# Two fused blocks on one core: one root for two norms, weights split ahead, and the residual's norm moved into the output projection

## The reference, cut to what matters

```python
# end of first_block
x = x + hier_moe(rmsnorm(x, g_ffn), ...)     # 1024 tokens, 1024 features
x = rmsnorm(x, g_final)                      # the "middle" norm
# start of second_block, layer 0
h = rmsnorm_2(x, norm_g[0]) * (1.0 + scale) + shift
proj = h @ w_in[0]                           # many column groups
...                                          # four branches -> y
x = x + gate * (y @ w_out[0])                # needs the normed x of above
```

## Time and profile before

| | before |
|---|---|
| median of 3 runs | 3914.94 us (3911.86 to 3916.8) |
| the profiled execution: time / span | 3911.92 us / 3910.1 us |
| PE busy with matmuls | 3686.8 us, 94% of the span |
| DVE / ACT / POOL busy | 1949.0 / 1546.8 / 69.2 us |
| mean granted TensorE clock | 0.967 of full |
| moved by DMA | 473.83 MB, 121 GB/s over the span |

### The profile page before, as it was taken

One profiled execution on the slowest core, in us unless ns is written; L12 is line 12 of the kernel. 1 busy time (PEld: TensorE's weight loads), 2 busy tenths in 40 slices (PEclk: granted clock), 3 DMA queues, 4 the chain that ended last, 5 costly groups with the idle time before them and its releaser, 6 DMA issues.

```text
span 3910.1 us, 45141 instructions
## 1 busy us (share of the span) xinstructions
PE 3686.8 (94%) x18674; PEld 2905.4 (74%) x18674; DVE 1949.0 (50%) x2538; ACT 1546.8 (40%) x1798; POOL 69.2 (2%) x54
## 2 busy tenths in 40 slices
PE   7999999989999986999999999999999998999998
PEld 5876767766666653777888888787777887788777
DVE  4454544355555534564556653434564456653334
ACT  4331112345555534432455632433433455533333
POOL 0000000000000001000000000000000000000000
PEclk9999999989999997999999999999999999999999
DMA  5101543389999964011101111432010101011232
GB/s 188 44 25 49 174 141 124 111 301 369 373 370 370 367 238 151 29 37 36 54 31 49 35 58 38 151 135 92 33 44 33 55 23 49 33 55 44 104 139 97
DMA packets 92019, 473.83 MB, mean 121 GB/s; under 512 B 10128, under 2 KB 10768, under 8 KB 53920
## 3 DMA queue, kind: packets, MB, share of 16 engines
q1 hardware_dynamic: 77072, 416.32, 29.0%
q0 software_dynamic: 8976, 33.56, 2.2%
q10 hardware_dynamic: 5760, 20.97, 1.3%
HBM read 414.19 MB, written 56.62 MB: 120 GB/s over the span
## 4 chain that ended last, share of the span: by engine, by line
PE 51%; DVE 5%; ACT 4%; issue 2%; ACTq 0%; DVEq 0%
PE ps L136 13%; PE ps L138 13%; PE ps L137 13%; PE ps L1654 3%; PE ps L315 1%; PE ps L1499 1%; PE ps L1479 1%; PE ps L1473 1%; PE ps L1442 1%; PE ps L1899 1%; PE ps L1638 1%; DVE WA L3452 1%; PE ps L3348 0%; PE ps L3381 0%; PE ps L3369 0%
## 5 line engine op out<-in xcount | busy, mean ns | idle before, releaser
L136 PE MATMUL ps<-HH,WS 128*128 128x512 f32 (+1 forms) x2608 | 1055.9, 405 | 25.6 <-DVE HL L3728 17.0
L138 PE MATMUL ps<-HH,WS 128*128 128x512 f32 (+1 forms) x2608 | 1026.6, 394 | 0.0
L137 PE MATMUL ps<-HL,WS 128*128 128x512 f32 (+1 forms) x1968 | 776.5, 395 | 0.0
L136 PEld LDWEIGHTS ps<-HH,WS 128*128 128x128 f32 (+1 forms) x2608 | 496.4, 190 | 156.1 <-issue 33.3
L138 PEld LDWEIGHTS ps<-HH,WS 128*128 128x128 f32 (+1 forms) x2608 | 494.4, 190 | 108.5
L1319 ACT ACTIVATE WA<-ps 128x512 f32<-128x512 f32 x240 | 143.1, 597 | 904.2 <-PE ps L138 794.6
L137 PEld LDWEIGHTS ps<-HL,WS 128*128 128x128 f32 (+1 forms) x1968 | 376.4, 191 | 79.4 <-issue 5.1
L1260 DVE TENSOR_TENSOR WS<-RAW,WS 128x1024 fp32r<-128x1024 f32 (+1 forms) x153 | 200.5, 1311 | 172.4 <-ACT WS L1255 172.3
L136 PE MATMUL ps<-WS,HH 128*128 128x256 f32 x896 | 263.3, 294 | 12.2 <-DVE HL L2131 12.2
L137 PE MATMUL ps<-WS,HH 128*128 128x256 f32 x896 | 256.0, 286 | 0.0
L138 PE MATMUL ps<-WS,HL 128*128 128x256 f32 x896 | 256.0, 286 | 0.0
(11 more groups left out here) (379 smaller groups left out, 5331.2 us busy)
## 6 DMA issues: line engine op xcount, KB each, us to landing
WR<-in_weu SPq DMA_DIRECT2D x37, 1024.0 KB
WR<-in_weg SPq DMA_DIRECT2D x35, 1024.0 KB
WR<-in_wed SPq DMA_DIRECT2D x34, 1024.0 KB
RAW<-in_wo SPq DMA_DIRECT2D x32, 1024.0 KB, 4.9
H<-in_wed SPq DMA_DIRECT2D x26, 1024.0 KB, 8.4
WA<-in_wada SPq DMA_DIRECT2D x48, 512.0 KB
H<-in_weg SPq DMA_DIRECT2D x23, 1024.0 KB, 7.8
H<-in_weu SPq DMA_DIRECT2D x21, 1024.0 KB, 6.4
```

What stands on the lines that cost most here:

```text
L136: t.matmul(o, l[0], r[0], start=st, stop=False)
L137: t.matmul(o, l[0], r[1], start=False, stop=False)
L138: return t.matmul(o, l[1], r[0], start=False, stop=sp)
```

## The change

It has these parts, in order of the program.

1. Routing: the sums of squares of `ffn` are issued one place earlier in PE's list (the sixth ahead of the last product, the seventh ahead of `tensor_row(t, 0)`); `hot` and `places` of k = 1 get the tiles of `PL` and `wrt`. DVE gets 4 instructions for the gains (`vector_gains`) and the bounds in three steps: at the end of the gates, ahead of the wait for the second half of the table, and after expert 0's splits. ACT's bounds stand ahead of expert 0's `start`.
2. The layer's first weights: the rooms `RAW` and `WS` are given to layer 0 from the pieces' last use by expert 31, not from the end of the optional blocks (which keep 6 of the 11 pieces). Weights rows, x0 and x1 are split before the chunks are handled.
3. Between the blocks: squares of x' are taken per chunk (1 ACT instruction of 1024 columns), and the layer's root comes from sums weighted with `g_final`² + 1e-6 (`tensor_gain_sum`, 8 matmuls of 128 columns per chunk). The middle norm is no longer applied to `X`; its gain goes into the input's gain. Chunks 6 and 7 are handled after product rows of half 0.
4. The middle root itself is needed only for the output: its sums (`tensor_chunk_sum`, again 8 matmuls of 128 columns per chunk) stand inside product rows, after steps 1, 3, 5 and 7. Its root is made by ACT in `scalar_first` after product x0 of half 1, stored to DRAM (`r_scratch`), read back ahead of `X` in `output_sync`, and applied by DVE for k = 6 to 13 of half 0 of the output (2 instructions of 512 columns each).
5. Layer 1: the squares and the root of half 1 stand on ACT ahead of the copy of product x1 of half 0 (`scalar_input_root`), and a few tiles are taken later.

The core of the diff:

```diff
+        def vector_gains(v):
+            g = PV[:, P1["g_final"]:P1["g_final"] + 8]
+            v.tensor_tensor(GAIN, g, g, ALU.mult).then_inc(*up("gain_square"))
+            v.wait_ge(*at("gain_square"))
+            v.tensor_scalar(GAIN, GAIN, EPS, None, ALU.add)
+            v.wait_ge(*at("mod_done", 0))
+            v.tensor_tensor(INPUT_GAIN, MD[:, 24:32], g, ALU.mult)
+            v.tensor_scalar(EPS2, eps, EPS, None, ALU.mult).then_inc(*up("gains"))
+        def tensor_gain_sum(t, c):
...
+            t.wait_ge(*at("squared", "mid", c))
+            for k in range(8):
+                o = t.matmul(ps("rms", ("l", 0), c // 4)[:, c % 4 * 128:(c % 4 + 1) * 128],
+                             GAIN[:, k:k + 1].broadcast_to([128, 128]), c8(tl("sq", "mid", c))[:, k, :], start=k == 0, stop=k == 7)
...
+        def scalar_middle_root(a):
+            r = tl("r", "mid")
+            free(a, wa, "r", "mid")
+            for i in range(2):
+                a.wait_ge(*at("sq_summed", "mid", 4 * i + 3))
+                a.activation(half(r, i), ps("rms", "mid", i), ACT.Ln, scale=1.0 / 1024, bias=eps).then_inc(*up("rms_ln", "mid", i))
+            a.wait_ge(*at("rms_ln", "mid", 1))
+            a.activation(r, r, ACT.Exp, scale=-0.5).then_inc(*up("rms", "mid"))
 # routing_room / moe_plan
-            for k in range(2):
-                for n, nm in enumerate(("hot", "places")):
-                    wa.take_piece(wa.has["stg", 2 - 2 * k + n], nm, k)
+            for n, nm in enumerate(("hot", "places")):
+                wa.take_piece(wa.has["stg", 2 + n], nm, 0)
...
+            early = dict(loose.free)
+            raws.free = [(i, early[i] + early[i + 1]) for i in range(2)]
+            wss.free = [(i, early[3 + i]) for i in range(2)]
+            loose.free = [(n, ends) for n, ends in loose.free if n > 4]
 # moe_tensor
+            for c in range(4):
+                tensor_turned_back(t, c)
+                if c:
+                    tensor_gain_sum(t, c - 1)
+            tensor_gain_sum(t, 3)
+            tensor_turned_back(t, 4)
+            tensor_turned_back(t, 5)
+            tensor_gain_sum(t, 4)
+            tensor_gain_sum(t, 5)
 # moe_scalar
-            bounds_scalar(a)
-            scalar_split(a, 0, 0)
-            a.wait_ge(*at("x_moe", 3, 1))
-            for k in range(8):
-                scalar_square(a, "mid", k, 0)
-            scalar_root(a, "mid", 0)
...
+            for _, n in first_tiles(0):
+                scalar_split(a, 0, n)
+            for c in range(4):
+                scalar_chunk_square(a, c)
+            scalar_first_root(a, 0)
+            for c in (4, 5):
+                scalar_chunk_square(a, c)
 # moe_vector, after the splits of rows, x0, x1
+            vector_added(v, 0)
+            for c in (1, 2, 3):
+                vector_added(v, c)
+                vector_moved(v, c - 1)
+            vector_moved(v, 3)
+            vector_added(v, 4)
+            vector_added(v, 5)
+            vector_moved(v, 4)
+            vector_moved(v, 5)
 # tensor_first
-                if i:
+                if i and layer:
                     for k in range(8):
                         tensor_square_sum(t, ("l", layer), k, 1)
                 for x, (_, n) in enumerate(tiles):
+                    tensor_half(t, layer, n, i, ready=None if x else lambda k, i: ("h_lo", layer, k, i),
+                                between=() if x or layer else range(4 * i, 4 * i + 4))
+                    if layer == 0 and i == 0:
+                        for c in (6, 7):
+                            if x == 0:
+                                tensor_turned_back(t, c)
+                            elif x == 1:
+                                tensor_gain_sum(t, c)
 # scalar_first
+                    elif (i, x) == (0, 2):
+                        if layer:
+                            scalar_input_root(a, layer)
+                        else:
+                            scalar_first_root(a, 1)
...
                     if x:
                         scalar_half(a, layer, n, i, ("u", U, x - 1))
                     if (i, x) == (1, 1):
+                        if layer == 0:
+                            scalar_middle_root(a)
 # sync: store at (i, x) == (1, 2), read back ahead of X
+                        s.dma_start(rd, tl("r", "mid")).then_inc(*up("r_out", by=16))
+                s.dma_start(tl("rb"), rd).then_inc(*up("r_back", by=16))
 # output_vector
+                    if layer == 0 and i == 0 and 5 < k < 14:
+                        middle(k - 6)
```

More of the change, by code:

```diff
@@ new lines, in tensor_chunk_sum, with scalar_first_root @@
+        def tensor_chunk_sum(t, c):
+            if c % 4 == 0:
+                free(t, banks, "rms", "mid", c // 4)
+            for k in range(8):
+                o = t.matmul(ps("rms", "mid", c // 4)[:, c % 4 * 128:(c % 4 + 1) * 128], ones, c8(tl("sq", "mid", c))[:, k, :],
+                             start=k == 0, stop=k == 7)
+            o.then_inc(*up("sq_summed", "mid", c))
+        def scalar_first_root(a, i):
+            r = half(tl("r", ("l", 0)), i)
+            if i == 0:
+                free(a, wa, "r", ("l", 0))
+                a.wait_ge(*at("gains"))
+            a.wait_ge(*at("gain_sum", 4 * i + 3))
+            a.activation(r, ps("rms", ("l", 0), i), ACT.Ln, scale=1.0 / 1024, bias=EPS2).then_inc(*up("rms_ln", ("l", 0), i))
+            a.wait_ge(*at("rms_ln", ("l", 0), i))
+            a.activation(r, r, ACT.Exp, scale=-0.5).then_inc(*up("rms", ("l", 0), i))
@@ L342, in moe_plan @@
             brief("table", end=("tab_gate",))
-            wa.give(("PL",), ("dest",))
+            for nm, key, end in (("hot", ("PL",), ("dest",)), ("places", ("wrt",), ("hT_turn", 7, 1))):
+                wa.give(key, end)
+                wa.take_piece(wa.has[key], nm, 1)
             wa.give(("R",), ("gates",), ("stg", 7, 1))
-            for key in (("r", "ffn"), ("wrt",)):
-                wa.give(key, ("hT_turn", 7, 1))
+            wa.give(("r", "ffn"), ("hT_turn", 7, 1))
             wa.give(("EH",), ("hot", 1))
@@ L1293, in tensor_pass, with tensor_half @@
                 yield
-        def tensor_half(t, layer, n, i, right=lambda k, hs: (HH[:, k, hs], HL[:, k, hs]), ready=None):
+        def tensor_half(t, layer, n, i, right=lambda k, hs: (HH[:, k, hs], HL[:, k, hs]), ready=None, between=()):
             hi, lo = parts(layer, n)
@@ L3688, in x_ready @@
         def x_ready(layer, k, i):
-            return ("x_new", 0, k, i) if layer else ("normed", "mid", k, i)
+            return ("x_new", 0, k, i) if layer else ("x_moe", 4 * i + 3, 1)
         def h_of(layer, k, i):
@@ L3733, in vector_input @@
             if i == 0:
-                v.wait_ge(*at("mod_done", layer))
+                v.wait_ge(*(at("mod_done", layer) if layer else at("gains")))
+            gain = md[:, 24:32] if layer else INPUT_GAIN
             for k in range(8):
@@ L3761, in output_plan @@
                 wa.take("yl", layer, *load_key(q))
+            if layer == 0:
+                wa.take("rb")
+                wa.give(("rb",), ("x_mid", 7, 1))
             ysr.free = [(i, (("pj_mm", layer, LAST[layer], 1),)) for i in range(4)]
@@ L3969, in layer_plan @@
                 plan_split(1, 0)
-            plan_input(layer, 1)
             plan_units(layer)
@@ L3976, in layer_sync @@
             sync_raw(s, layer, 1)
-            sync_split(s, layer, 0)
             if layer == 0:
+                for _, n in first_tiles(0):
+                    sync_split(s, 0, n)
                 sync_input(s, 0, 0)
+            else:
+                sync_split(s, 1, 0)
             sync_input(s, layer, 1)
```

227 lines of the change are left out of this document (137 added, 90 removed).

## The result

The changed kernel takes **3883.9 us** (median of four runs, 3882.7 to 3888.4) against 3915.9 of the kernel before on the same chip (3911.9 to 3919.6): ratio 0.9921, 95% interval 0.9903 to 0.9938. Forecast were 3876 and a range of 3865 to 3890. Ten microseconds of the gain are missing between the profiled executions, and the task of the experiments is to say where.

The account below looks back on a forecast made before the run. PE was full where matmuls stream, but not between the last expert and layer 0. There -38.3, middle root +3.5, routing -2.8 and layer 1 -1.3 sum to -38.9: median 3914.9 to 3876, range 3865 to 3890.

Parts of the forecast that it names:

- Weights ahead, -4.9: Before layer 0: loads start earlier, so the last store travels alone, landing at 1459.6; gathers start at 1460.5, 4.9 earlier.
- rival B: The early loads don't free the last store, gathers start at 1465 as before: +4.9, 3881; chance 0.1.
- Chunks and root of half 0: Between the blocks: chunk work overlaps, root done at 1490.2, HL's first tile at 1496.7 after X's stores.
- rival A: Clock stays low up to and into product rows, PE working between waits for gathers: 3884 to 3886; chance 0.15.
- Product rows 13.5: Between the blocks: with four chunk sums PE is slower than DVE, so rows take 13.5 us per half, not 10.6.
- rival E: The sums stay and set the pace both before and after, time near 3915; chance 0.02.
- D: Clock doesn't return in product rows, as PE waits for DVE: 55 us more, 3931; chance 0.03.
- Middle root, +3.5: Half 1 of layer 0: the 4.9 us root on ACT makes x1's copy 3.5 late, and the next split with it.
- Routing, -2.8: Ahead of the experts: root 0.9 earlier, `hot` wait gone, PE 2.1 more; indices written at 801.8, not 804.7.
- the debit that I had named: Routing: ahead of the indices DVE now waits for ACT's first Ln of the bounds, put at 801.4.
- Layer 1, -1.3: Input of half 1: squares now lie ahead of the copy of x1, 1.4 us, for a gain of 1.3.
- Output of layer 0, 0: 16 added DVE instructions of 0.66 spread over 8 PE steps of 5.4 us cost nothing.

Follow-up runs that it names:

- held loads: Layer 0's first raw weight loads wait again for the last product of the last block's output, otherwise the changed kernel: 3886.2 us.
- First profile: The changed kernel's first profiled execution, no edit: 3883.0 us, against 3911.92 for the profiled execution of the kernel before.
- Third profile: Third profiled execution of the changed kernel, no edit; its timed runs beside two variants have a median of 3881.8 us.
- repeated run: The changed kernel profiled once more, no edit: 3881.9 us.
- last of the timed kernels: Root and loads later: changed kernel with middle root one square later and first input loads ahead of the second pair of weight loads: median 3877.0 us.
- routing undone: Changed kernel with the seventh tile's sum back behind the eighth's output product and hot and places in old buffers; bounds and gains kept: 3879.3 us.
- kept-busy one: Changed kernel plus 26 products into a bank nobody reads, filling TensorE's waits in the gather phase: 3877.5 us.
- small Ln: Changed kernel plus one small Ln on ScalarE ahead of the four chunk squares, to load the root's table early: 3880.6 us.
- the same kernel: Changed kernel with the middle root issued one square later, behind the copy of x1 of half 1: 3871.5 us profiled, 3881.7 median timed.

## Why the prediction was right, and where it was off

The sign, the range and the mechanism held: the gain lies between the blocks, from chunks that overlap and one root less on the path. By its steps, in the profiled execution, forecast -38.9, measured -29.0 between the spans (28.9 between the times):

- **Weights ahead, -4.9: right in cause, too large.** -3.1 by experiment. A store's traffic is over after 2.6 us, but the waiting engine goes on 4.1 to 4.4 us after the issue; I priced the bytes, not the end of the wait. The first gather stood 5.0 us behind the issue, more than the 4 that I had named as the sign of rival B; still B is excluded, by the held loads. (The rate of the old gathers should read 0.35 MB/us, 9.4 MB in 26.9 us, not 0.37; the sum used 0.35.)
- **Chunks and root of half 0: the step that failed most.** Forecast: root done at 1490.2, HL's first tile at 1496.7, product rows from about 1496.8. First profile: 1498.1, 1500.7, 1504.2. Third profile, without the unknown wait: 1493.7, 1497.0, 1500.0. HL's wait for X, which was forecast with 2 us, is there with 1.8, and it swallowed the later root. What failed are two sizes: the root takes 4.0, since its table is loaded behind the wait and not ahead of it; and I left the sums of chunks 4 and 5 no place on PE ahead of rows. They take 5.4 us at half clock, after a wait of 3.37 of PE. That is rival A in small: the clock did come up for the first sums, and fell again between root and rows. The unknown wait, 4.1, came on top in the profile that is compared, as much as 3.6 of it reaching the end (a difference of gather to split; 1.0 against the repeated run).
- **Product rows 13.5: right** for half 0 (12.9), and 14.9 for half 1, where PE's wait of 2.29 was followed by a clock of half for the first sum (2.65, not 1.95). Together the stretch gave 30.7 in place of 38.3. That excludes rival E, and the clock of 0.89 and then 1.00 in the first 20 us of rows and x0 (1500 to 1520) excludes D.
- **Middle root, +3.5: right**, 3.4 by experiment, with PE's wait of 4.8 as forecast. That the lost wait would shorten the whole was wrong in the timed runs.
- **Routing, -2.8: only in part, and the clock took the rest.** Counted as in the experiment, the root (773.49, before 773.53) starts 0.8 earlier, as forecast (0.9). The wait of `hot` went too, but of the 2.1 behind it 0.5 came. Moving the seventh tile's sum ahead of the last output product left PE with a longer wait ahead of the matmuls that rank the picks, and those then ran at half clock (0.66 granted from 785 to 790, 1.00 before). The kernel before, the changed one, and the last of the timed kernels:

```profile
784.43 0.72 PE L785 MATMUL ps<-WA,CT 128*128 128x288 f32 x2 [1.78 <-DVE WA L980]
784.99 2.38 PE L788 MATMUL ps<-WA,CT 128*128 128x256 f32 x16
```

```profile
784.40 0.72 PE L873 MATMUL ps<-WA,CT 128*128 128x288 f32 x2 [3.43 <-DVE WA L1062]
784.96 4.04 PE L876 MATMUL ps<-WA,CT 128*128 128x256 f32 x16
```

```profile
788.32 0.72 PE L873 MATMUL ps<-WA,CT 128*128 128x288 f32 x2 [3.44 <-DVE WA L1062]
788.88 2.38 PE L876 MATMUL ps<-WA,CT 128*128 128x256 f32 x16
```

  4.04 in place of 2.38 us: 1.7 lost, for rows, ACT's copies and DVE's list behind them. So ACT's last row copies came at 793.83 (before 792.21), 0.9 later when the late start is taken off, and with them the first Ln of the bounds, for which DVE then stands:

```profile
803.93 0.16 DVE L1835 SCALAR_TENSOR_TENSOR LB<-SM 128x4 f32<-128x4 f32 x1 [4.77 <-ACT SM L1841]
804.29 0.20 DVE L1142 TENSOR_SCALAR WA<-ps 128x48 int32<-128x48 f32 x1
```

  Forecast 801.4 and 801.8. The removed wait gave its place to the debit that I had named, 2.5 us later than I had put it (0.8 of it the late start, 1.7 the clock). The matmuls took 4.0 us in ten of the twelve executions with the 3.4 us wait and 2.38 in two, the kept-busy one and the profiled one of root and loads later; in the routing undone the wait is 1.78 and they take 2.38. In those two executions the half-clock spell in expert 1 is absent as well, expert 0's first product starts 2.9 and 2.2 us earlier than before, and the last expert still ends 2.4 and 2.3 us earlier (692.1 and 692.3, before 694.5). So the -2.8 was nearly right where the clock held, and an earlier start does last through the experts. In the first profile the clock left 0.5 of the 1.3 at the end of the experts, and that execution had begun 0.8 late.
- **Layer 1, -1.3:** 1.6. From the first rounded tile of half 0 to that of half 1 it is 79.55 us before and 77.96 or 77.97 in all thirteen profiles behind the change. **Output of layer 0, 0:** right, the lead over before is 26.7 on both sides of it.

The Trainium skill ("ScalarE: Activation LUTs", "Table sets: the hidden batching unit") has ln and exp in one set. The rows above show a load ahead of each (L370, L372), also behind the small Ln, where only the first was saved. The trace disagrees here too.

## What to carry to other kernels

Price the clock with every wait that an edit adds to the main engine's path or takes from it: behind a wait of 3.4 us the same two sums took 5.3 to 5.4 us in nine of ten executions, behind one of 2.1 us 3.8 in both; and in the routing an edit that took work off the path made a wait of 1.8 us one of 3.4 and, in ten of twelve executions, lost 1.7 to the clock behind it. Judge an edit of a few microseconds by stretches between the same instructions of two traces, one of which here repeats within 0.05 us, but claim it only from timed runs beside each other: 3.4 us shown locally were nothing in the time. And a DMA share of 0.98 is no proof of a transfer bound; adding work to each engine in turn tells in one run.

## What the runs showed that I had not expected

- The clock takes back what was won elsewhere, far away, in steps of about 1.6 or 3.2 us: the same kernel took 3871.5 us on one chip, where the changed one took 3881.9, and 3881.7 on another, where the changed one took 3881.8.
- DVE stood 2.3 to 4.1 us without a releaser of the program at an addition of a chunk to X in four of fourteen executions, not always at the same chunk.
- A table load that stands before a waiting activation runs ahead of the wait in half 1 (1525.00, activation at 1527.90) but behind it in half 0 (1494.17, behind 4.39 of waiting).
- 256 KB more per expert at a DMA share of 0.98 cost nothing: 19.90 us per expert, share 1.00.
